# Turning the expert loop of a mixture-of-experts decoder layer by half an item, and loading two weight slices one step sooner

## The chip, the cores and the metric

The kernel runs on one core of a Trainium2 chip. The metric is device time of one execution in microseconds (us). The kernel before took 1735.72 us (median of 3 runs, 1734.24 to 1736.85).

## What is computed

One decoder layer on 512 tokens of width 1024: an attention part (two groups of heads, not touched here), and then a mixture of experts. Each token goes to 4 of 32 experts:

```
logits = h @ w_router + b_router
top_val, top_exp = lax.top_k(logits, TOP_K)          # TOP_K = 4
gate_w = jax.nn.softmax(top_val, axis=-1)
...
gt = jnp.minimum(xb @ w_gate[e] + b_gate[e], SWIGLU_LIMIT)
up = jnp.clip(xb @ w_up[e] + b_up[e], -SWIGLU_LIMIT, SWIGLU_LIMIT)
return (gt * jax.nn.sigmoid(SWIGLU_ALPHA * gt) * (up + 1.0)) @ w_down[e] + b_down[e]
```

The weighted results are added up per token, and a layer norm follows. `w_gate`, `w_up` and `w_down` are 1024 x 1024 float32 for each expert, 12 MB per expert.

## The kernel before

**Items.** The pairs of token and expert are cut into items of up to 32 rows of one expert; in this run there are 82 items. Items with an even number use side A of the weight ring, those with an odd number side B; each side holds the three matrices of one expert. A planner on VectorE fills small tables: `land_i` (which load, in order, an item needs), `perm_i`, `done_i`, `done7_i`, `base_i` (for each load: the expert, the item that uses the slots last, the same in units of `s_gu`, the side), and `ends_i` (the number of items and of pairs of items).

**TensorE** runs per item, written out in this order: eight slices `gate_up` k = 0 to 7 (line 1062), with the bias (line 1056) after k = 0; the transposes of the activations after k = 3; `down` slices q = 0 and 1 of the item before, after k = 5; then k = 6 and 7; then `next_rows`: the transposes of the gathered rows (line 1041) and `slots`, four small matmuls (line 1035); then `down` q = 2 and 3 of the item before (line 1084). The loop (line 1152) has two items in its body and turns around between k = 7 and `next_rows`. `land(m)` (line 1114) reads one number of `land_i` from SBUF into a register of TensorE's sequencer; it stands once ahead of q = 2 (only in the first of the two items), once ahead of k = 0 (in both), and once ahead of q = 0 (first item).

**SyncE** issues all weight loads from one in-order queue. For each load x from 2 on it reads four table values, waits until the slots' last user has passed k = 1 (`s_gu` at `done7`), issues the bias of gate and up (line 460), and then gate and up slices (line 449), each as far as its slot is free, then waits for `down` q = 1, issues the bias of down and the four down slices (line 454).

**GpSimd** issues, for each item, an indirect gather of its rows (line 659) and an indirect scatter that adds its result in DRAM (line 675). Ahead of the loop stand two scatters whose indices all lie out of bounds (`nowhere`, line 666), which stand in for the items 'before the first'; the second waits until the first has landed (`s_sc` at 16). Their order with the first gathers is gather, nowhere, gather, nowhere, gather.

**VectorE and ScalarE** do the activation, the slot values and the row copies of each item. The first gather needs `s_idx`, set at line 1781; the scatters ahead of the loop need `s_tables`, set at line 1754.

Of the kernel before, what the change touches and what calls it, by code (L numbers as in the profile page):

```python
# [12 lines left out]
KC = D // P  # L13
# [8 lines left out]
NE = 32  # L22
# [27 lines left out]
NX = 128  # L50
# [9 lines left out]
def build_layer(nc, a, out):  # L60
    f32, bf16, i32, u32 = mybir.dt.float32, mybir.dt.bfloat16, mybir.dt.int32, mybir.dt.uint32
    ALU, ACT, AX = mybir.AluOpType, mybir.ActivationFunctionType, mybir.AxisListType
    ds = bass.ds
    ctx = ExitStack()
    with ctx:
# [289 lines left out]
        def _(sp):  # L355
# [87 lines left out]
            def gate_up_load(k, e, first, m):  # L443

                dst = arena[:, row_of(first, 2 * k + m), :]
                if type(first) is not int:
                    dst = dst.rearrange("p a n -> p (a n)")
                src = a["w_up" if m else "w_gate"][0, e, k * P:(k + 1) * P, :]
                sp.dma_start(dst, src.rearrange("a p n -> p (a n)")).then_inc(s_wg[k], 16)
# [88 lines left out]
            with sp.Fori(2, NE) as x:  # L538
                e = ds(sp.value_load(perm_i[0:1, ds(x, 1)], min_val=0, max_val=NE - 1), 1)
                done = sp.value_load(done_i[0:1, ds(x, 1)], min_val=1, max_val=NX)  # L540
                done7 = sp.value_load(done7_i[0:1, ds(x, 1)], min_val=8, max_val=7 * NX + 1)
                b = sp.value_load(base_i[0:1, ds(x, 1)], min_val=0, max_val=1)
                first = b * 24
                sp.wait_ge(s_bg, x * 16)
                sp.wait_ge(s_gu, done7)
                bias_load(s_bg, 0, 512, e, ds(b, 1))
                for k in range(KC):
                    if k == KC - 1:
                        sp.wait_ge(s_a, done)
                    elif k > 1:  # L550
                        sp.wait_ge(s_gu, done7 + (k - 1))
                    sp.wait_ge(s_wg[k], x * 32)
                    for m in range(2):
                        gate_up_load(k, e, first, m)
                sp.wait_ge(s_dn, done * 3 + 1)
                sp.wait_ge(s_bd, x * 16)
                bias_load(s_bd, 512, 768, e, ds(b, 1))
                for q in range(4):
                    if q == 3:
                        sp.wait_ge(s_c, done + 1)  # L560
                    elif q > 1:
                        sp.wait_ge(s_dn, done * 3 + q)
                    sp.wait_ge(s_wd[q], x * 16)
                    down_load(q, e, first)
# [12 lines left out]
        def _(pool):  # L577
# [75 lines left out]
            def gather(ready, free):  # L653

                pool.wait_ge(s_idx, ready)
                if free is not None:
                    pool.wait_ge(s_tx, free)
                pool.sem_inc(s_past, 1)
                pool.indirect_dma_start(xg, None, h2_d, bass.IndirectOffsetOnAxis(ap=idx_g, axis=0),  # L659
                                        bounds_check=4 * T - 1, oob_is_err=False).then_inc(s_g, 16)  # L660

            def nowhere(before):

                if before:
                    pool.wait_ge(s_sc, 16 * before)
                pool.indirect_dma_start(acc_d, bass.IndirectOffsetOnAxis(ap=idx_s, axis=0), yb, None,
                                        bounds_check=4 * T - 1, oob_is_err=False, compute_op=ALU.add).then_inc(s_sc, 16)
# [11 lines left out]
            pool.wait_ge(s_zst, 16 * QT)  # L679
            pool.wait_ge(s_zero, 1)  # L680
            pool.wait_ge(s_tables, 1)
            gather(1, None)
            nowhere(0)
            gather(2, 1)
            nowhere(1)
            gather(3, 2)
            n_items = pool.value_load(ends_i[0:1, 0:1], min_val=NE, max_val=NX)
            with pool.Fori(1, n_items) as m:
# [8 lines left out]
        def _(pe):  # L697
# [355 lines left out]
            def gate_up_bias(b):  # L1053

                for j in range(4):
                    nc.tensor.matmul(bank[0][strip(j), :], selp[:, j, :], brow[32:44, b, 0:512], start=False, stop=False)
# [51 lines left out]
            for k in range(KC):  # L1108
                gate_up(0, k, 64 if k >= 4 else 32)
                if k == 0:  # L1110
                    gate_up_bias(0)

            def land(m):
                return pe.value_load(land_i[0:1, ds(m, 1)], min_val=0, max_val=NE - 1)

            def next_rows(m):

                pe.wait_ge(s_g, m * 16 + 32)
                rows_transposed()
                pe.wait_ge(s_oh, m + 3)  # L1120
                pe.wait_ge(s_idx, m + 2)
                slots()

            def gate_up_begins(b, m, at):

                pe.wait_ge(s_urd, m)
                pe.wait_ge(s_bg, at * 16 + 16)
                pe.wait_ge(s_xe, m + 1)
                gate_up(b, 0, at * 32 + 32)
                gate_up_bias(b)  # L1130
                for k in (1, 2, 3):
                    gate_up(b, k, at * 32 + 32)
                activations_transposed(m + 1)
                for k in (4, 5):
                    gate_up(b, k, at * 32 + 32)

            def second_half(b, m, at, at1):
                down_begins(1 - b, at1 * 16 + 16, m, m + 1)
                for k in (6, 7):
                    gate_up(b, k, at * 32 + 32)  # L1140

            def rest_of_down(b, at):
                for q in (2, 3):
                    down(b, q, at * 16 + 16)
            next_rows(0)
            gate_up_begins(1, 1, 1)
            down_begins(0, 16, 1, 2)
            for k in (6, 7):
                gate_up(1, k, 64)
            n_items = pe.value_load(ends_i[0:1, 0:1], min_val=NE, max_val=NX)  # L1150
            n_pairs = pe.value_load(ends_i[0:1, 1:2], min_val=NE // 2, max_val=NX // 2)
            with pe.Fori(1, n_pairs) as i:
                next_rows(i * 2 - 1)
                rest_of_down(0, land(i * 2 - 2))
                at = land(i * 2)
                gate_up_begins(0, i * 2, at)
                at1 = land(i * 2 - 1)
                second_half(0, i * 2, at, at1)
                next_rows(i * 2)
                rest_of_down(1, at1)  # L1160
                after = land(i * 2 + 1)
                gate_up_begins(1, i * 2 + 1, after)
                second_half(1, i * 2 + 1, after, at)
            pe.wait_ge(s_g, n_items * 16 + 16)
            rows_transposed()
            pe.wait_ge(s_oh, n_items + 2)
            pe.wait_ge(s_idx, n_items + 1)
            slots()
            for q in (2, 3):
                down(0, q, 16 * NE)  # L1170
            activations_transposed(n_items + 1)
            down_begins(1, 16 * NE, n_items, n_items + 1)
            for q in (2, 3):
# [198 lines left out]
        def _(dve):  # L1372
# [365 lines left out]
            nc.vector.tensor_scalar(colsb[:, 2:3], start, -1.0, None, ALU.add)  # L1738
            nc.vector.tensor_copy(colsb[:, 3:4], second)
            nc.vector.scalar_tensor_tensor(WP[:, 0:NX], parity, second, Wf, ALU.is_equal, ALU.mult).then_inc(s_selb, 1)  # L1740
            nc.vector.tensor_copy(ends_i[0:1, 1:2], pairs[0:1, :])
            nc.vector.tensor_scalar(ends_i[0:1, 0:1], pairs[0:1, :], 2.0, None, ALU.mult)
            nc.vector.memset(val, 0.0)
            nc.vector.memset(backv, 0.0)
# [4 lines left out]
            nc.vector.tensor_scalar(perm_i[0:1, :], bank[6][0:1, 64 + NX:64 + NX + NE], float(NE), None, ALU.add)  # L1749
            nc.vector.tensor_copy(land_i[0:1, :], bank[6][0:1, 224:224 + NX])  # L1750
            nc.vector.tensor_copy(done_i[0:1, :], bank[6][0:1, 384:416])
            nc.vector.tensor_scalar(done7_i[0:1, :], bank[6][0:1, 384:416], 7.0, 1.0, ALU.mult, ALU.add)
            nc.vector.tensor_copy(base_i[0:1, :], bank[6][0:1, 416:448])
            nc.vector.scalar_tensor_tensor(posr[:, :, 0:NE], bank[5][:, 128:160].unsqueeze(1).to_broadcast([P, QT, NE]), 16.0, cum4,
                                           ALU.mult, ALU.add).then_inc(s_tables, 1)
# [51 lines left out]
            slot_values(2, 3)  # L1807
            one_hot(expert_of(slice(2, 3)))
            n_items = dve.value_load(ends_i[0:1, 0:1], min_val=NE, max_val=NX)
            def body(m, landed):  # L1810
                dve.wait_ge(s_a, m + 1)
                dve.wait_ge(s_pr, m + 1)
                nc.vector.tensor_scalar(gcl, bank[0][:, 0:256], 7.0, None, ALU.min).then_inc(s_gdr, 1)  # L1813
                dve.wait_ge(s_act, m + 1)
                nc.vector.tensor_scalar(ucl, bank[0][:, 256:512], 8.0, -6.0, ALU.min, ALU.max).then_inc(s_urd, 1)
                dve.wait_ge(s_gdr, m + 1)
                dve.wait_ge(s_sig, m + 1)
                nc.vector.tensor_tensor(sgm, gcl, sgm, ALU.mult).then_inc(s_pr, 1)  # L1818
                dve.wait_ge(s_urd, m + 1)
                dve.wait_ge(s_pr, m + 2)  # L1820
                nc.vector.tensor_tensor(sgm, sgm, ucl, ALU.mult).then_inc(s_act, 1)
                moved_on(m + 2, m + 2, m * 2 + 4, m + 1)
                slot_values(m + 3, m * 2 + 5)
                e = expert_of(ds(m + 3, 1))
                one_hot(e)
                dve.wait_ge(s_c, m + 1)
                scatter_indices(m + 3, landed)
            body(0, 32)
            with dve.Fori(1, n_items) as m:
                body(m, m * 16 + 16)  # L1830
                weighted(m + 3, m * 16 + 16)
            moved_on(n_items + 2, n_items + 2, n_items * 2 + 4, n_items + 1)
            scatter_indices(n_items + 3, n_items * 16 + 16)
# [67 lines left out]
```

## Time and profile before

| | |
|---|---|
| median of 3 runs | 1735.72 us |
| the profiled execution | 1734.24 us |
| its span, first to last instruction | 1732.4 us |
| what lies around the span | 1.84 us |
| TensorE busy | 1501.7 us, 87% of the span |
| mean granted TensorE clock | 0.914 of full |
| DMA | 488.94 MB, 282 GB/s over the span |

Times in rows are in us from the span's start unless marked ns. PE is TensorE's matmul, PEld its weight load (LDWEIGHTS), PEldq its sequencer (register, branch and table-load instructions), SPq SyncE's queue. A row names line, engine, operation, what it writes and reads, and the number of instructions. The engine rows by stretch give busy time with the number of instructions in brackets, the granted TensorE clock, the mean busy share of the 16 DMA engines and their GB/s.

### The profile page before, as it was taken

Reading aid. Unit: us, or ns where it says so; the run is one execution under the profiler, and the core shown is the slowest. Engines: PE = TensorE matmul, PEld = TensorE weight load, DVE = VectorE, ACT = ScalarE, POOL = GpSimd, SP = SyncE. Lnnn points to the kernel's source line nnn. Section 1 sums busy time; section 2 is a strip of 40 time slices with the busy share of each in tenths; the row PEclk is TensorE's granted clock in tenths of the full one; section 3 lists DMA queues with packets and bytes.
Section 4 is the critical chain, followed back from the end, with each engine's and each line's share of the span. In section 5 each row is a group of like instructions: output and inputs, shape, how many; then the busy total and the mean of one; then the engine's idle time right before and its main releaser. Section 6 shows DMA issues by size and latency. Waiting matters only on the chain. (4 is left out here: it accounts for less than half of the span.)

```text
span 1732.4 us, 39655 instructions
## 1 busy us (share of the span) xinstructions
PE 1501.7 (87%) x14019; PEld 601.1 (35%) x14020; DVE 623.0 (36%) x2318; ACT 250.7 (14%) x690; POOL 293.8 (17%) x220
## 2 busy tenths in 40 slices
PE   6999989889749966887889997997999998979783
PEld 4444445444413311222233332332333332323221
DVE  1147874655843310221222231331323331313224
ACT  1012265640100000000000000000011000000002
POOL 0010000114411210111121221121222121211111
PEclk9999989989769986998999998998999997979897
DMA  9721246831465999999998799769979869395994
GB/s 345 190 73 49 80 159 249 259 126 79 179 269 200 405 402 408 405 402 403 363 390 302 263 363 404 288 257 404 378 281 343 303 239 375 102 403 177 403 404 162
DMA packets 178905, 488.94 MB, mean 282 GB/s; under 512 B 40375, under 2 KB 59891, under 8 KB 177844
## 3 DMA queue, kind: packets, MB, share of 16 engines
q1 hardware_dynamic: 162740, 471.63, 70.9%
q0 software_dynamic: 16128, 16.82, 4.8%
q8 instruction: 22, 0.36, 0.1%
q14 instruction: 15, 0.12, 0.0%
HBM read 474.60 MB, written 17.96 MB: 284 GB/s over the span
## 5 line engine op out<-in xcount | busy, mean ns | idle before, releaser
L1062 PE MATMUL banks<-arena,master 128*32 128x512 f32 x5248 | 682.8, 633 | 129.0 <-DMA arena<-in_w_up 127.3
L1084 PE MATMUL banks<-arena,master 128*32 128x256 f32 x5248 | 340.0, 389 | 3.4 <-DVE master L1793 2.5
L1813 DVE TENSOR_SCALAR master<-banks 128x256 f32<-128x256 f32 x82 | 34.8, 424 | 798.4 <-PE banks L1062 798.4
L1062 PEld LDWEIGHTS banks<-arena,master 128*32 128x32 f32 x5248 | 149.9, 112 | 431.5 <-DMA arena<-in_w_up 211.7
L659 POOL DMA_INDIRECT master<-moe_input,misc x84 | 93.3, 1110 | 919.0 <-DVE misc L1781 865.7
L1084 PEld LDWEIGHTS banks<-arena,master 128*32 128x32 f32 x5248 | 156.7, 112 | 144.6 <-issue 61.8
L675 POOL DMA_INDIRECT moe_output<-master,misc x82 | 130.2, 1587 | 100.4 <-issue 96.7
L1337 ACT ACTIVATE master<-banks 128x256 f32<-128x256 f32 x82 | 31.4, 383 | 565.7 <-PE banks L1071 565.7
L824 PE MATMUL banks<-arena 128*128 128x512 f32 x256 | 112.6, 595 | 0.0
L1332 ACT ACTIVATE master<-master 128x256 f32<-128x256 f32 x82 | 34.2, 416 | 535.8 <-DVE master L1813 535.8
L1761 DVE TENSOR_SCALAR master<-cbias 128x128 bf16<-128x128 f32 x340 | 95.0, 343 | 44.5 <-issue 44.0
L824 PEld LDWEIGHTS banks<-arena 128*128 128x128 f32 x256 | 47.9, 190 | 60.5 <-issue 59.4
L1515 DVE CUSTOM_DVE_ANT_0 arena<-banks,master 128x128 f32<-128x128 f32 (+3 forms) x96 | 46.0, 480 | 63.4 <-PE banks L912 62.8
L1286 ACT ACTIVATE arena<-arena,misc 128x128 f32<-128x128 f32 (+3 forms) x96 | 53.1, 554 | 61.9 <-DVE misc L1515 61.9
L984 PE MATMUL banks<-arena 128*128 128x512 f32 x128 | 57.5, 607 | 1.5 <-DVE arena L1609 1.5
L922 PE MATMUL banks<-cst,arena 128*128 128x128 f32 x240 | 41.6, 311 | 13.7 <-ACT arena L1294 13.2
L912 PE MATMUL banks<-arena 64*128 64x128 f32 (+3 forms) x192 | 44.0, 538 | 3.5 <-DVE misc L1515 3.2
L1041 PE MATMUL banks<-cst,master 128*128 128x128 f32 x166 | 36.6, 303 | 8.2 <-DMA master<-moe_input,misc 8.2
L1041 PEld LDWEIGHTS banks<-cst,master 128*128 128x128 f32 x166 | 16.8, 141 | 77.0 <-issue 68.7
L1071 PEld LDWEIGHTS banks<-cst,master 128*128 128x128 f32 x164 | 17.0, 145 | 74.9 <-issue 74.5
L922 PEld LDWEIGHTS banks<-cst,arena 128*128 128x128 f32 x240 | 29.3, 156 | 37.9 <-issue 25.7
L1818 DVE TENSOR_TENSOR master<-master 128x256 f32<-128x256 f32 x82 | 34.8, 425 | 18.1 <-ACT master L1332 18.1
(311 smaller groups left out, 1268.1 us busy)
## 6 DMA issues: line engine op xcount, KB each, us to landing
arena<-in_w_gate SPq DMA_DIRECT2D x256, 512.0 KB, 11.7
arena<-in_w_up SPq DMA_DIRECT2D x256, 512.0 KB, 13.9
arena<-in_w_down SPq DMA_DIRECT2D x128, 1024.0 KB, 15.4
arena<-in_w_ada SPq DMA_DIRECT2D x12, 2048.0 KB, 13.2
arena<-in_x SPq DMA_DIRECT2D x2, 2048.0 KB, 8.6
arena<-in_w_in SPq DMA_DIRECT2D x2, 2048.0 KB, 9.9
master<-bias_by_distance SPq DMA_DIRECT2D x16, 256.0 KB, 5.0
arena<-in_w_in SPq DMA_DIRECT2D x8, 256.0 KB, 4.3
```

The source lines that it names most:

```text
L659: pool.indirect_dma_start(xg, None, h2_d, bass.IndirectOffsetOnAxis(ap=idx_g, axis=0), bounds_check=4 * T - 1, oob_is_err=False).then_inc( ...
L675: pool.indirect_dma_start(acc_d, bass.IndirectOffsetOnAxis(ap=idx_s, axis=0), yb, None, bounds_check=4 * T - 1, oob_is_err=False, compute_ ...
L824: last = nc.tensor.matmul(b[:, :], w_in[:, k, where:where + P], hT[:, k, :], start=(k == 0), stop=(k == KC - 1))
L912: nc.tensor.matmul(bank[(2 * s + half) % 3][:, 0:n], lhs, rhs, start=not masked, stop=True).then_inc(s_S, 1)
L922: last = nc.tensor.transpose(bank[3 + half][:, kb * P:(kb + 1) * P], Sb[:, s % 4, half, kb * P:(kb + 1) * P], ident)
L984: last = nc.tensor.matmul(bank[1 + 2 * (q % 2) + n][:, :], mixT[:, k, q * P:(q + 1) * P], w_out[:, k, n * 512:(n + 1) * 512], start=(k == ...
L1041: last = nc.tensor.transpose(bank[2][:, c * P:(c + 1) * P], xg[:, c * P:(c + 1) * P], ident)
L1062: last = nc.tensor.matmul(two(bank[0][strip(j), :]), hTe[:, k % 2, strip(k // 2)], arena[:, 24 * b + 2 * k:24 * b + 2 * k + 2, quarter(j)] ...
L1084: last = nc.tensor.matmul(bank[1][strip(j), 0:256], actT[:, c, strip(q)], DN(b, q, c)[:, quarter(j)], start=(q == 0 and c == 0), stop=(q = ...
L1286: nc.scalar.activation(Sb[:, s % 4, u % 2, 0:n], Sb[:, s % 4, u % 2, 0:n], ACT.Exp, scale=-1.0, bias=umin[:, u:u + 1], accum_out=usum[:, u ...
L1515: nc.vector.tensor_tensor_reduce(out=Sb[:, s % 4, half, 0:n], in0=bank[u % 3][:, 0:n], in1=biases, scale=1.0, scalar=3e38, op0=ALU.add, op ...
L1761: nc.vector.tensor_scalar(OH[:, q, :].rearrange("p (j t) -> p j t", j=4), iota4, posr[:, q, e], backv, ALU.subtract, ALU.is_equal)
```

## The change

- TensorE's loop is turned: it now goes around between `down` q = 3 and `gate_up` k = 0, with the bodies in one function `item_body`. The order of the matmuls is the same as before. Both table reads of an item now stand at its head, ahead of k = 0. The loop goes over one pair less, and the last item stands behind it; three register values are read ahead of the loop.
- SyncE issues the first gate slice of a load as soon as k = 0 is used, then up's; the bias and k = 1 follow once k = 1 is used. The first down slice goes out once `down` q = 0 is used, ahead of the bias of down.
- GpSimd issues both `nowhere` scatters ahead of the first gather.
- `ends_i` gets a third value (one more small VectorE instruction), and the first body of VectorE's item loop waits for one landed scatter and not two.

```diff
-                done7 = sp.value_load(done7_i[0:1, ds(x, 1)], min_val=8, max_val=7 * NX + 1)
+                done7 = sp.value_load(done7_i[0:1, ds(x, 1)], min_val=7, max_val=7 * NX)
                 b = sp.value_load(base_i[0:1, ds(x, 1)], min_val=0, max_val=1)
                 first = b * 24
+                sp.wait_ge(s_wg[0], x * 32)
+                sp.wait_ge(s_gu, done7)
+                gate_up_load(0, e, first, 0)
                 sp.wait_ge(s_bg, x * 16)
-                sp.wait_ge(s_gu, done7)
+                gate_up_load(0, e, first, 1)
+                sp.wait_ge(s_gu, done7 + 1)
                 bias_load(s_bg, 0, 512, e, ds(b, 1))
-                for k in range(KC):
+                for k in range(1, KC):
                     if k == KC - 1:
                         sp.wait_ge(s_a, done)
                     elif k > 1:
-                        sp.wait_ge(s_gu, done7 + (k - 1))
+                        sp.wait_ge(s_gu, done7 + k)
                     sp.wait_ge(s_wg[k], x * 32)
                     for m in range(2):
                         gate_up_load(k, e, first, m)
+                sp.wait_ge(s_dn, done * 3)
+                sp.wait_ge(s_wd[0], x * 16)
+                down_load(0, e, first)
                 sp.wait_ge(s_dn, done * 3 + 1)
                 sp.wait_ge(s_bd, x * 16)
                 bias_load(s_bd, 512, 768, e, ds(b, 1))
-                for q in range(4):
+                for q in range(1, 4):
...
+            for n in range(2):
+                nowhere(n)
             gather(1, None)
-            nowhere(0)
             gather(2, 1)
-            nowhere(1)
             gather(3, 2)
...
+            n_items = pe.value_load(ends_i[0:1, 0:1], min_val=NE, max_val=NX)
+            n_whole = pe.value_load(ends_i[0:1, 1:2], min_val=NE // 2 - 1, max_val=NX // 2 - 1)
+            n_last = pe.value_load(ends_i[0:1, 2:3], min_val=NE - 1, max_val=NX - 1)
+
+            def item_body(m, b):
+
+                land = pe.value_load(land_i[0:1, ds(m, 1)], min_val=0, max_val=NE - 1)
+                back = pe.value_load(land_i[0:1, ds(m - 1, 1)], min_val=0, max_val=NE - 1) * 16 + 16
+                here = land * 32 + 32
+                pe.wait_ge(s_urd, m)
+                pe.wait_ge(s_bg, land * 16 + 16)
+                pe.wait_ge(s_xe, m + 1)
+                gate_up(b, 0, here)
+                gate_up_bias(b)
+                for k in (1, 2, 3):
+                    gate_up(b, k, here)
+                activations_transposed(m + 1)
+                for k in (4, 5):
+                    gate_up(b, k, here)
+                down_begins(1 - b, back, m, m + 1)
+                for k in (6, 7):
+                    gate_up(b, k, here)
                 pe.wait_ge(s_g, m * 16 + 32)
                 rows_transposed()
                 pe.wait_ge(s_oh, m + 3)
                 pe.wait_ge(s_idx, m + 2)
                 slots()
...
                 for q in (2, 3):
-                    down(b, q, at * 16 + 16)
...
+                    down(1 - b, q, back)
+            with pe.Fori(0, n_whole) as i:
+                item_body(i * 2 + 1, 1)
+                item_body(i * 2 + 2, 0)
+            item_body(n_last, 1)
...
-            nc.vector.tensor_copy(ends_i[0:1, 1:2], pairs[0:1, :])
+            nc.vector.tensor_scalar(ends_i[0:1, 1:2], pairs[0:1, :], -1.0, None, ALU.add)
+            nc.vector.tensor_scalar(ends_i[0:1, 2:3], pairs[0:1, :], 2.0, -1.0, ALU.mult, ALU.add)
...
-            def body(m, landed):
+            def body(m):
...
-                scatter_indices(m + 3, landed)
-            body(0, 32)
+                scatter_indices(m + 3, m * 16 + 16)
+            body(0)
```

## Rows read from the trace of the kernel before

**Rows 1.** The page: busy time by engine, and the costliest group of instructions.

```profile
PE 1501.7 (87%) x14019; PEld 601.1 (35%) x14020; DVE 623.0 (36%) x2318; ACT 250.7 (14%) x690; POOL 293.8 (17%) x220
...
L1062 PE MATMUL banks<-arena,master 128*32 128x512 f32 x5248 | 682.8, 633 | 129.0 <-DMA arena<-in_w_up 127.3
```

**Rows 2.** Engines by stretch, in stretches with long waits for weights.

```profile
542.00:857.00 315.00, 252.78 (x2628) 82.79 (x2624) 72.92 (x324) 21.43 (x72) 48.75 (x37) 0.88 1.03 403
...
1029.00:1086.00 57.00, 45.50 (x496) 14.97 (x488) 12.16 (x54) 3.57 (x12) 8.22 (x7) 0.88 1.03 398
```

**Rows 3.** Engines by stretch, just before such stretches begin.

```profile
538.00:540.00 2.00, 2.00 (x24) 0.67 (x24) 1.54 (x8) 0.00 (x0) 1.10 (x1) 1.00 0.00 0
862.00:864.00 2.00, 2.00 (x28) 0.52 (x20) 1.40 (x10) 0.00 (x0) 0.16 (x1) 1.00 0.32 131
```

**Rows 4.** Timeline of TensorE's matmuls, one item.

```profile
1021.75 0.24 PE L1035 MATMUL banks<-cbias,master 128*128 128x6 bf16 x4
1021.93 1.93 PE L1084 MATMUL banks<-arena,master 128*32 128x256 f32 x32
1023.68 1.04 PE L1062 MATMUL banks<-arena,master 128*32 128x512 f32 x8
1024.65 0.39 PE L1056 MATMUL banks<-misc,cst 12*32 12x512 bf16 x4
1024.97 1.07 PE L1062 MATMUL banks<-arena,master 128*32 128x512 f32 x8
...
1033.98 0.24 PE L1035 MATMUL banks<-cbias,master 128*128 128x6 bf16 x4
```

**Rows 5.** Timeline of SyncE's queue in the same item.

```profile
1026.34 0.38 SPq L460 DMA_DIRECT2D misc<-bias_parts  x1
1027.02 0.37 SPq L449 DMA_DIRECT2D arena<-in_w_gate  x1
```

**Rows 6.** TensorE's sequencer (by line) and weight loads (timeline), the same item.

```profile
L1152 PEldq ALU_OP  x1: 32/32/32, 1019.2 to 1019.2; - x1
...
L1152 PEldq FUSED_REGOPS  x1: 68/68/68, 1019.6 to 1019.6; - x1
...
L1114 PEldq FUSED_REGOPS  x2: 51/101/151, 1022.4 to 1022.9; - x2
L1114 PEldq TENSOR_LOAD <-cst x1: 297/297/297, 1022.5 to 1022.5; - x1
...
L1060 PEldq FUSED_REGOPS  x1: 37/37/37, 1023.4 to 1023.4; - x1
...
1021.92 1.45 PEld L1084 LDWEIGHTS banks<-arena,master 128*32 128x32 f32 x32
1023.46 0.35 PEld L1062 LDWEIGHTS banks<-arena,master 128*32 128x32 f32 x8
```

**Rows 7.** Line 1056 in two stretches without waits for weights (four matmuls per item).

```profile
L1056 PE MATMUL banks<-misc,cst x36: 383/385/386, 926.8 to 1024.7; 12*32 12x512 bf16 x36
...
L1056 PE MATMUL banks<-misc,cst x64: 383/385/386, 1215.9 to 1399.4; 12*32 12x512 bf16 x64
```

**Rows 8.** Timelines of VectorE, GpSimd and TensorE as the expert stage begins.

```profile
487.99 0.27 DVE L1754 SCALAR_TENSOR_TENSOR cbias<-banks,arena 128x128 f32<-128x128 f32 x1
490.81 0.20 DVE L1781 TENSOR_SCALAR misc<-cbias 128x1 f32<-128x1 f32 x1
...
492.12 1.24 POOL L659 DMA_INDIRECT master<-moe_input,misc  x1 [28.53 <-issue]
...
498.57 0.69 PE L1041 MATMUL banks<-cst,master 128*128 128x128 f32 x2 [8.19 <-DMA master<-moe_input,misc]
```

**Rows 9.** Line 666, the two scatters ahead of the loop.

```profile
L666 POOL DMA_INDIRECT moe_output<-master,misc x2: 1587/1596/1604, 493.7 to 502.3; - x2
...
DMA to landing us min/median/max: 7.0/7.3/7.7
```

**Rows 10.** Line 675, the 82 scatters of the items: time to landing.

```profile
DMA to landing us min/median/max: 3.2/7.4/9.0
```

More of the change, by code:

```diff
@@ L1111, in _ @@
                     gate_up_bias(0)
-            def land(m):
-                return pe.value_load(land_i[0:1, ds(m, 1)], min_val=0, max_val=NE - 1)
-            def next_rows(m):
+            pe.wait_ge(s_g, 32)
+            rows_transposed()
+            pe.wait_ge(s_oh, 3)
+            pe.wait_ge(s_idx, 2)
+            slots()
+            n_items = pe.value_load(ends_i[0:1, 0:1], min_val=NE, max_val=NX)
[18 more added lines that the diff above has]
+                    gate_up(b, k, here)
                 pe.wait_ge(s_g, m * 16 + 32)
@@ L1122, in next_rows @@
                 slots()
[L1124 to L1142, printed above, removed]
-                for q in (2, 3):
-                    down(b, q, at * 16 + 16)
[L1145 to L1170, printed above, removed]
+                for q in (2, 3):
+                    down(1 - b, q, back)
[3 more added lines that the diff above has]
+            item_body(n_last, 1)
             activations_transposed(n_items + 1)
@@ L1751, in _ @@
             nc.vector.tensor_copy(done_i[0:1, :], bank[6][0:1, 384:416])
-            nc.vector.tensor_scalar(done7_i[0:1, :], bank[6][0:1, 384:416], 7.0, 1.0, ALU.mult, ALU.add)
+            nc.vector.tensor_scalar(done7_i[0:1, :], bank[6][0:1, 384:416], 7.0, None, ALU.mult)
             nc.vector.tensor_copy(base_i[0:1, :], bank[6][0:1, 416:448])
@@ L1826, in body @@
                 dve.wait_ge(s_c, m + 1)
-                scatter_indices(m + 3, landed)
-            body(0, 32)
+                scatter_indices(m + 3, m * 16 + 16)
+            body(0)
             with dve.Fori(1, n_items) as m:
-                body(m, m * 16 + 16)
+                body(m)
                 weighted(m + 3, m * 16 + 16)
```

## The prediction

> **What bounds the kernel now.** I read the page first: TensorE is busy for 1501.7 of 1732.4 us, and its costliest line, the gate and up matmuls, also has the largest wait, 129 us, for weights [rows 1]. So the expert stage is bound by TensorE in one place and by DMA in another, and the second view, the engines by stretch, has to say where. There are seven stretches in which the DMA share stands at 1.03 and TensorE is not fully busy; the first and longest runs from 542 to 857 us, the others (868 to 922, 1029 to 1086, 1155 to 1213, 1404 to 1461, 1506 to 1563, 1596 to 1684) last 54 to 88 us; two of the seven are shown [rows 2]. In them time is set by bytes: what TensorE does sooner or later inside changes nothing. Just before six of the seven the DMA engines stand idle, share 0.00 to 0.02; before the one at 865 they still have 0.32 to do [rows 3]. So such a stretch begins when SyncE's first load goes out, and ends a fixed number of bytes later. Between them TensorE is gapless and sets the pace: an item takes 1033.98 - 1021.75 = 12.23 us [rows 4]. The total is therefore the sum of TensorE-paced stretches and DMA-paced ones, and a change has to be priced by which kind it falls in.
>
> The line of the small bias matmul, four per item, counts the items in TensorE-paced stretches: 36/4 = 9 from 921 to 1027 and 64/4 = 16 from 1211 to 1402 [rows 7]; the same count gives 6 (1085 to 1153), 4 (1460 to 1503), 3 (1562 to 1593), 1 near 863, 1 at 1688, and 2 beside the very first in the loop before 540. That is 42 passages from `down` q = 3 to k = 0 of the next item, 21 ahead of an odd item and 21 ahead of an even one (I followed the parity from the loop's branch, which now runs ahead of even items).
>
> **SyncE's order.** The wait for k = 1 ends at 1024.97 + 1.07 = 1026.04; the bias goes out at 1026.34 and the first gate slice at 1027.02 [rows 4, 5]. With the change the first gate slice needs only k = 0, which ends at 1023.68 + 1.04 = 1024.72, and no bias ahead of it: 1.32 us sooner by the wait and 1027.02 - 1026.34 = 0.68 us by the bias, 2.0 us in all. The next slices don't fall behind: k = 0 and up's k = 0 are 1 MB, over 2.5 us at 403 GB/s [rows 2], and the bias and k = 1 follow within 2.0 us. Six of the seven DMA-paced stretches begin dry, so 6 x 2.0 = 12.0 us. The one at 865 begins while a part of the engines still works on old loads: between 0 and 2.0, taken as 1.0. The other loads are issued behind a queue that is full, and gain nothing; so does the down slice that goes out ahead of its bias, which at that time has gate and up slices queued ahead of it. Queued behind SyncE's new wait on the old bias is only its own next slice; that bias was issued a whole load earlier. Sum: -13.0 (bounds -14 and 0: below 0 only if the stretch doesn't begin with this slice).
>
> **TensorE's loop.** The matmuls and their order stay. What moves is sequencer work: a table read (a register operation, a load of 297 ns, register operations of 151 ns) runs from 1022.4 to about 1023.1, 0.7 us, and going around the loop runs from 1019.2 to 1019.67, 0.5 us [rows 6]. It is hidden as long as matmuls are queued ahead. Going around now happens behind k = 6 and 7, whose matmuls last long; it moves behind `down` q = 2 and 3, whose 32 last 1023.68 - 1021.93 = 1.75 us in all, 55 ns each [rows 4]. How much is still queued there? When the table read begins at 1022.4, the weight loads of `down` still run until 1021.92 + 1.45 = 1023.37, and the first weight load of k = 0 comes at 1023.46, right behind the sequencer's last register operation for it at 1023.4 [rows 6]. So one table read and the waits just fit, and nothing is left over. The second read adds 0.7 us to every passage. Of this 0.22 us is covered, because now the weight load at 1023.46 leads its matmul at 1023.68 by that much: 0.48 us exposed. Ahead of odd items the turn of the loop adds 0.47: 0.95 to 1.0, taken as 0.98. Sum: 21 x 0.48 + 21 x 0.98 = 30.7 us. Bounds: 0 if the queue can hold more; 21 x 0.7 + 21 x 1.2 = 39.9 if the 0.22 us isn't cover. I take the first because the sequencer began the read 0.97 us before the loads of `down` ran out, not sooner, although nothing else kept it. In DMA-paced stretches the same idle time lies inside waits for weights. Nothing is gained where the loop turned before: there it was covered.
>
> A row shows the depth: at 1022.4 about (1023.37 - 1022.4)/0.045 = 21 weight loads and, at 55 ns a piece since 1021.93, 23 matmuls were outstanding, 45 instructions [rows 4, 6]. The Trainium skill (TensorE: Matmul & The Clock Gate, Part 1, on queue depths) gives TensorE's queue as 64 deep. By that rule all 64 instructions of `down` q = 2 and 3 would be queued when it starts at 1021.93, 0.47 us sooner than the trace has the read begin; the trace does not agree, and I go by the trace, but keep the rule's result as a rival.
>
> **GpSimd's order.** The first gather needs `s_idx`, which comes at 490.81 + 0.20 = 491.01; it starts at 492.12, 1.1 us later, and TensorE, idle for 8.19 us, starts at 498.57, 6.45 us after that [rows 8]. No wait is longer in this chain, so the first gather's time passes on in full until the first DMA-paced stretch, and past it, since its start hangs on TensorE's k = 0. Now: tables at 488.26, first `nowhere` 1.1 us later at 489.4; it lands 7.3 us after its start, at 496.7 (these two took 7.0 and 7.7) [rows 8, 9]; the second waits for that, starts 1.1 us later at 497.8, runs 1.6 us to 499.4, and the gather starts some 0.6 us behind it at 500.0. That is 7.9 us late. Bounds: with the shortest landing of any scatter, 3.2 us [rows 10], it is 3.8 us; with 7.7 and a slower hand-over 8.9. The down loads that slow the landing start at the same moment, so I keep 7.3. What is late next is TensorE's first transpose. The second gather gains nothing, since it waits for that transpose.
>
> **VectorE.** The third value of `ends_i` is one instruction on one partition, ahead of a wait of VectorE for TensorE (`s_pos`) that it cannot outlast; the wait for one scatter instead of two is long past. Nothing for both. The three register reads ahead of TensorE's loop run while it waits for the row copy: 0 to 0.5 us, taken as 0.
>
> **Sum,** against the profiled execution's own 1734.24 us (span 1732.4 and 1.84 around it; the median of the runs is 1.5 us above it): 1734.24 - 13.0 + 30.7 + 7.9 = 1759.8 us.
>
> **Rivals.**
> 1. *TensorE's queue hides all of it.* If the sequencer could run further ahead than 1.0 us, by more than 0.7 us at even items and 1.2 at odd ones, the loop costs nothing, and 1734.24 - 13.0 + 7.9 = 1729.1 us: faster. The place is k = 0 of each item; it turns the sign as soon as the mean exposure falls below 5.1/42 = 0.12 us. Against it: the weight load at 1023.46 directly behind the register operation [rows 6].
> 2. *A queue of 64.* The read begins 0.47 us sooner, so the exposures fall to 0.01 and 0.51: 21 x 0.52 = 10.9 us, and 1740.0 us. The skill's page named above has this depth.
> 3. *The early slices don't help* (DMA-paced stretches are held by something other than their first byte, a slow engine among the 16, say): 13.0 us more, 1772.8 us. For it: the uneven end before 865 [rows 3]. Against it: idle engines before the other six.
> 4. *The scatter lands fast:* 1755.7 us. Inside the range of the forecast.
>
> **How the numbers follow.** The forecast 0.62, rival 1 0.13, rival 2 0.12, rival 3 0.13 (rival 4 is part of the first). The forecast's own range is 1749 to 1771, from both ends of the exposure and of the landing. For 8 in 10 it has to reach to rival 2 and part of rival 3, and leave out rival 1: 1738 to 1774. What can be told from no change is 0.2%, 3.5 us about the median 1735.7. Faster: rival 1, 0.12. Same: the rest of rival 1 and the low end of rival 2, 0.06. Slower 0.82.
>
> **What the changed profile would show.** Items in TensorE-paced stretches at 12.7 and 13.2 us in turn in place of 12.23; TensorE idle ahead of k = 0, put down to issue, with both table reads in the gap. SyncE's first gate slice about 0.3 us after k = 0 and 2.0 us sooner against the item. The first gather near 500 us and TensorE's first transpose near 506. The DMA-paced stretches as long as before. I would be wrong if the items still take 12.23 us, if the first `nowhere` lands by 493, or if the waits for weights grow by as much as SyncE starts sooner.

## The result, and the profile after

The changed kernel takes 1762.71 us (median of 4 runs, 1762.42 to 1765.37) against 1734.98 us, 27.7 us more: ratio 1.016, 95% interval 1.0144 to 1.0174. It is slower, and lies 2.9 us above the forecast of 1759.8. Its profiled execution took 1760.31 us with a span of 1758.5.

On the page, TensorE's busy time is as before. The view by line gives three causes of idle time for each group. TensorE's idle time ahead of the gate and up matmuls is 147.8 us and was 129.0 [rows 1]. It was nearly all put down to weights (127.3); now weights are 64.7, and 41.6 is put down to issue (time in which the engine waited for nothing that the profile shows) and 40.5 to the bias:

```profile
PE 1503.2 (85%) x14015; PEld 593.0 (34%) x14020; DVE 621.9 (35%) x2319; ACT 250.7 (14%) x690; POOL 294.1 (17%) x220
...
L1069 PE MATMUL banks<-arena,master 128*32 128x512 f32 x5248 | 674.3, 627 | 147.8 <-DMA arena<-in_w_up 64.7 <-issue 41.6 <-DMA misc<-bias_parts 40.5
```

TensorE's timeline shows it at k = 0 (line 1069, after `down` at 1091), once ahead of an odd item and once ahead of an even one; the brackets give the idle time and its cause:

```profile
1019.54 0.24 PE L1042 MATMUL banks<-cbias,master 128*128 128x6 bf16 x4
1019.72 1.93 PE L1091 MATMUL banks<-arena,master 128*32 128x256 f32 x32
1022.51 1.07 PE L1069 MATMUL banks<-arena,master 128*32 128x512 f32 x8 [0.86 <-issue]
...
1032.84 0.24 PE L1042 MATMUL banks<-cbias,master 128*128 128x6 bf16 x4
1033.02 1.93 PE L1091 MATMUL banks<-arena,master 128*32 128x256 f32 x32
1035.19 1.07 PE L1069 MATMUL banks<-arena,master 128*32 128x512 f32 x8 [0.24 <-issue]
```

From the small matmuls of one item to those of the next it is now 13.30 us (1019.54 to 1032.84) and then 12.68, where it was 12.23 [rows 4]. From `down` q = 2 to k = 0 it is 2.79 and 2.17 us, where it was 1.75. The sequencer's rows ahead of the second of these have both table reads (lines 1130 and 1131) in one row, where there was one [rows 6]:

```profile
L1130 PEldq FUSED_REGOPS  x2: 51/101/151, 1033.5 to 1034.0; - x2
L1130 PEldq TENSOR_LOAD <-cst x1: 296/296/296, 1033.6 to 1033.6; - x1
...
L1131 PEldq TENSOR_LOAD <-cst x1: 296/296/296, 1034.2 to 1034.2; - x1
...
L1131 PEldq SEQ_ASSERT  x1: 18/18/18, 1034.8 to 1034.8; - x1
```

The first still begins 0.7 us after the small matmuls (1033.5 against 1032.84; before it was 1022.4 against 1021.75), so the sequencer runs as far ahead as before, and the work added behind that point comes out as idle time. Ahead of the other k = 0, at 1022.51, the turn of the loop (line 1153) also begins 0.7 us after the small matmuls. The sequencer's last register operation ahead of k = 0 (line 1067) comes 2.2 us after that, where it is 1.6 us without the turn (1033.5 to 1035.1); this is the 0.6 us between the two kinds of item:

```profile
L1153 PEldq ALU_OP  x1: 32/32/32, 1020.2 to 1020.2; - x1
...
L1067 PEldq FUSED_REGOPS  x1: 37/37/37, 1022.4 to 1022.4; - x1
...
L1067 PEldq FUSED_REGOPS  x1: 42/42/42, 1035.1 to 1035.1; - x1
```

SyncE's queue at the same k = 0, and GpSimd's timeline as the expert stage begins (line 673 is `nowhere`, 666 the gather) [rows 5, 8]:

```profile
1036.55 0.36 SPq L449 DMA_DIRECT2D arena<-in_w_gate  x1
1037.19 0.35 SPq L449 DMA_DIRECT2D arena<-in_w_up  x1
1037.84 0.37 SPq L460 DMA_DIRECT2D misc<-bias_parts  x1
```

```profile
488.81 1.77 POOL L673 DMA_INDIRECT moe_output<-master,misc  x1 [25.64 <-DVE cbias L1741]
496.61 1.56 POOL L673 DMA_INDIRECT moe_output<-master,misc  x1 [6.03 <-DMA moe_output<-master,misc]
498.47 1.08 POOL L666 DMA_INDIRECT master<-moe_input,misc  x1 [0.30 <-issue]
```

The first gate slice goes out 1036.55 - 1035.19 = 1.36 us after k = 0 begins; before it was 1027.02 - 1023.68 = 3.34. GpSimd waits 6.03 us between the two scatters. In the DMA-paced stretches the DMA share and the rate are as before, 1.03 and about 400 GB/s [rows 2]:

```profile
547.00:861.00 314.00, 248.56 (x2642) 81.48 (x2636) 72.92 (x324) 21.93 (x74) 49.42 (x37) 0.92 1.03 403
1039.00:1096.00 57.00, 48.78 (x506) 15.48 (x502) 12.16 (x54) 4.07 (x14) 9.35 (x7) 0.88 1.03 396
```

### The profile page after: what moved, and what is told of

Its sections match the earlier page's. It is cut to its first block and busy times, and to the rows that moved or that the text cites. A ratio compares the mean times of both kernels' runs of the same rounds, so it can differ in the third digit from the quotient of the medians.

```text
span 1758.5 us, 39756 instructions
## 1 busy us (share of the span) xinstructions
PE 1503.2 (85%) x14015; PEld 593.0 (34%) x14020; DVE 621.9 (35%) x2319; ACT 250.7 (14%) x690; POOL 294.1 (17%) x220
## 5 line engine op out<-in xcount | busy, mean ns | idle before, releaser
L1069 PE MATMUL banks<-arena,master 128*32 128x512 f32 x5248 | 674.3, 627 | 147.8 <-DMA arena<-in_w_up 64.7
L1069 PEld LDWEIGHTS banks<-arena,master 128*32 128x32 f32 x5248 | 142.8, 111 | 465.9 <-issue 263.9
L1091 PEld LDWEIGHTS banks<-arena,master 128*32 128x32 f32 x5248 | 156.3, 111 | 141.5 <-issue 59.6
L1272 ACT ACTIVATE arena<-arena,misc 128x128 f32<-128x128 f32 (+3 forms) x96 | 53.1, 554 | 61.7 <-DVE misc L1501 61.7
```

The lines of the kernel that those rows point to most:

```text
L1069: last = nc.tensor.matmul(two(bank[0][strip(j), :]), hTe[:, k % 2, strip(k // 2)], arena[:, 24 * b + 2 * k:24 * b + 2 * k + 2, quarter(j)] ...
L1091: last = nc.tensor.matmul(bank[1][strip(j), 0:256], actT[:, c, strip(q)], DN(b, q, c)[:, quarter(j)], start=(q == 0 and c == 0), stop=(q = ...
L1272: nc.scalar.activation(Sb[:, s % 4, u % 2, 0:n], Sb[:, s % 4, u % 2, 0:n], ACT.Exp, scale=-1.0, bias=umin[:, u:u + 1], accum_out=usum[:, u ...
```

## The experiments

Ten kernels were run against the kernel before, whose median was 1735.3 to 1735.9 us in these comparisons.

**SyncE's part alone** (the first part of the change's diff, with `done7_i` at 7 times `done`).

> The kernel before with SyncE's new order of issue alone. My theory: each of the seven DMA-paced stretches begins when the first gate slice goes out, so the gain is what the changed kernel's ledger shows for them without the one passage to k = 0 in each: -3.05 + 1.11 - 1.55 - 1.56 - 1.57 - 1.76 - 1.50 = -9.9 us, about 1725 us. Prediction's own term: -13.0 us, 1722 us. Rival (the wait for weights only moves elsewhere, and the ledger's gains come from the slower items, which give the DMA engines more time): 0 us, 1735 us. Items keep 12.23 us in all cases.

1727.11 us, ratio 0.9948 (0.9935 to 0.9961, which is 6.8 to 11.3 us): 8.2 us faster by the medians, where the prediction had 13.0 and the expectation 9.9. To see where the rest went I compared bytes at the same distance from an item's small matmuls, in the stretch that begins at 1155: 4 to 14 us behind them, and the 22 us after. First the kernel before (small matmuls at 1148.06), then SyncE's part alone (1146.82); the last number is GB/s:

```profile
1152.06:1162.06 10.00, 10.00 (x128) 3.95 (x124) 2.42 (x10) 1.19 (x4) 2.17 (x2) 1.00 0.76 247
1162.06:1184.06 22.00, 22.00 (x258) 7.75 (x250) 6.45 (x32) 1.69 (x6) 5.38 (x4) 1.00 1.04 403
```

```profile
1150.82:1160.82 10.00, 10.00 (x128) 3.98 (x124) 2.42 (x10) 1.19 (x4) 2.16 (x2) 1.00 0.94 315
1160.82:1182.82 22.00, 22.00 (x258) 7.71 (x250) 6.44 (x32) 1.70 (x6) 5.39 (x4) 1.00 1.03 403
```

In the first 10 us it is 3.15 MB against 2.47: 0.68 MB ahead, which at 403 GB/s is 1.7 us, and the lead stays, since afterwards both move 403. This pair of rows has one of the larger leads. Over all six dry starts (stretches that begin with idle DMA engines) the same 10 us hold 3.17 MB on average in the three kernels that have this part and the old loop (this one, without down slices, with one scatter), and 2.56 MB in four with SyncE's old order (before, GpSimd's part, unused read behind k = 7, one scatter first): 0.61 MB, 1.5 us.

What a dry start is worth in time is less again. I took the time from k = 0 of the item in which the loads begin to the small matmuls behind the stalled item (in the kernel before, for example, 1023.68 to 1086.71, 63.0 us), as a mean over the five short dry stretches of each profile:

| SyncE's order | kernels | mean of the five stretches, us |
|---|---|---|
| old | before; GpSimd's part; TensorE's part; its read late; unused read at k = 0; the same behind k = 7; one scatter first | 63.2; 62.5; 62.3; 62.4; 62.8; 62.9; 62.7 |
| new | changed kernel; SyncE's part; without down slices; with one scatter; changed kernel mended | 61.4; 61.7; 61.3; 61.3; 61.5 |

The means of the rows are 62.7 and 61.5 us, and the rows don't overlap: a dry start gains 1.2 us, not 2.0. Five are 6.2 us. The long stretch from 542, taken the same way, gains 0.9 on average, within the spread of the profiles, and what the stretch at 865 gives can't be told from that spread either. The table also bears out that a stretch set by bytes doesn't get longer when TensorE's items do (62.3 to 62.8 with slower items, 62.5 to 63.2 without).

The later slices show a like number. First the kernel before, then SyncE's part alone, each with the gate slices of k = 0 and k = 1:

```profile
1153.33 0.37 SPq L449 DMA_DIRECT2D arena<-in_w_gate  x1
...
1154.48 0.34 SPq L449 DMA_DIRECT2D arena<-in_w_gate  x1
```

```profile
1150.08 0.36 SPq L449 DMA_DIRECT2D arena<-in_w_gate  x1
...
1151.97 0.35 SPq L449 DMA_DIRECT2D arena<-in_w_gate  x1
```

Against the small matmuls the slice of k = 0 goes out at 5.27 and now 3.26 us, 2.0 us sooner, but that of k = 1 at 6.42 and now 5.15, only 1.3 us sooner: in the new order the wait until k = 1 is used, and the bias, stand between the two.

**SyncE's part without the down slices.**

```diff
-                sp.wait_ge(s_dn, done * 3)
-                sp.wait_ge(s_wd[0], x * 16)
-                down_load(0, e, first)
                 sp.wait_ge(s_dn, done * 3 + 1)
                 sp.wait_ge(s_bd, x * 16)
                 bias_load(s_bd, 512, 768, e, ds(b, 1))
-                for q in range(1, 4):
+                for q in range(4):
```

> SyncE's new order for the first gate and up slices and their bias alone; the down slices as before. Theory (the down slices go out into a queue that is full, so their order is worth nothing): the same as with both parts, 1727 us within 2 us. Rival (the down part carries some of the 8 us): 1729 us or more.

1726.32 us, ratio 0.9952 (0.994 to 0.9964). The down slices' new order shows no gain of its own; what is gained comes from the order of the first gate and up slices and their bias.

**GpSimd's part alone** (both `nowhere` ahead of the first gather).

> The kernel before with both out-of-bounds scatters ahead of the first gather, nothing else. Theory: the first gather comes 6.8 us later against the tables and TensorE's first transpose 6.2 us later; item 0 gets 1.4 us back if its clock rises sooner again, so +4.8 us in the end (1739.8 us). If the clock's rise was chance: +6.2. Rival (the delay is taken up by the first wait for weights at 590 us): 0.

1739.85 us, ratio 1.0025 (1.0016 to 1.0035): 4.6 us slower by the medians (2.8 to 6.1 by the interval). The delay of the start is not taken up by the later waits for weights.

**One scatter ahead of the first gather, one behind the second.**

```diff
-            gather(1, None)
             nowhere(0)
+            gather(1, None)
             gather(2, 1)
             nowhere(1)
```

> The kernel before with one out-of-bounds scatter ahead of the first gather and the second left in its place. Theory (the delay is the second scatter's wait for the first's landing, not the issuing): the scatter is over 2.8 us after the tables, just as the gather's indices are ready; the gather starts within 0.5 us of its old place against the tables, total within 1 us of before. Rival (each scatter ahead of the gather costs its share, half of the 4.6 us of both): +2.3 us.

1733.89 us, ratio 0.999 (0.998 to 0.9999): 1.7 us faster by the medians, a little more than the 1 us either way that was expected. GpSimd's timeline of this kernel:

```profile
488.99 1.78 POOL L666 DMA_INDIRECT moe_output<-master,misc  x1 [25.62 <-DVE cbias L1754]
491.69 1.09 POOL L659 DMA_INDIRECT master<-moe_input,misc  x1 [0.92 <-DVE misc L1781]
```

The scatter is over at 490.77 and the gather starts at 491.69, waiting for its indices as before. Issuing a scatter ahead of the gather costs nothing here; what costs is the second one's wait for the first to land.

**TensorE's part alone** (the turned loop and the third value of `ends_i`).

> The kernel before with TensorE's turned loop and the third value of the ends table alone. Theory: items in TensorE-paced stretches take 12.70 and 13.30 us in turn, 42 passages give 21 x 0.47 + 21 x 1.07 = 32.3 us, the three register reads ahead of the loop 0.95 us; together +33 us, 1768 us. Rival (the longer items are partly a matter of SyncE's new order, through semaphores or the queue): well under 33 us, items nearer 12.23.

1765.61 us, ratio 1.0175 (1.0162 to 1.0189, which is 28.1 to 32.8 us): 30.3 us slower, where 33 was expected. SyncE's order has no part in it; the items take 12.7 and 13.3 us here too. Item 1 takes 11.84 us against 11.60, so the register reads ahead of the loop cost 0.2 us here and not the 0.95 of the expectation.

**The same with the second table read under cover.**

```diff
-                back = pe.value_load(land_i[0:1, ds(m - 1, 1)], min_val=0, max_val=NE - 1) * 16 + 16
                 here = land * 32 + 32
...
                 for k in (4, 5):
                     gate_up(b, k, here)
+                back = pe.value_load(land_i[0:1, ds(m - 1, 1)], min_val=0, max_val=NE - 1) * 16 + 16
                 down_begins(1 - b, back, m, m + 1)
```

> As the run with TensorE's part alone, with the second table read moved from the head of the item to just ahead of down q = 0, where a long row of gate and up matmuls is queued. Theory (sequencer work beyond about 1.0 us at the head is exposed, one to one): even items back to 12.23 us, odd ones keep the turn of the loop only, 12.23 + 0.3 to 0.6; the sum 21 x (0.3 to 0.6) + 0.5 = 7 to 13 us, about 1745 us. Rival (a queue of 64, with the exposure due to something in the turned loop other than the reads, such as instruction fetch): little change from the 33 us.

1740.5 us, ratio 1.0032 (1.0019 to 1.0044): 5.2 us over the kernel before, less than the 7 to 13 expected. One line moved past six slices of matmuls takes 25 of 30 us away. The small matmuls of three items in a row:

```profile
1099.67 0.24 PE L1035 MATMUL banks<-cbias,master 128*128 128x6 bf16 x4
1112.16 0.24 PE L1035 MATMUL banks<-cbias,master 128*128 128x6 bf16 x4
1124.39 0.24 PE L1035 MATMUL banks<-cbias,master 128*128 128x6 bf16 x4
```

12.49 us and 12.23: one kind of item is back where it was, the other keeps 0.26 us for the turn of the loop. 21 x 0.26 = 5.5 us, close to the 5.2 measured.

**An unused read ahead of k = 0, in the kernel before**, whose loop is not turned:

```diff
                 at = land(i * 2)
+                land(i * 2 - 1)
                 gate_up_begins(0, i * 2, at)
...
                 after = land(i * 2 + 1)
+                land(i * 2)
                 gate_up_begins(1, i * 2 + 1, after)
```

> The kernel before, nothing turned; one more table read, whose value is not used, stands behind the one that already stands ahead of k = 0 in both items of the loop. Theory (one read and the waits just fit into what is queued of down, a second is exposed): every TensorE-paced item takes 12.70 us in place of 12.23, 42 passages give 42 x 0.47 = 19.7 us, about 1755 us. Rival (a queue of 64, and what is exposed in the changed kernel comes from its turned code): 0 to 0.5 us in all, 1735 us.

1755.68 us, ratio 1.0123 (1.0108 to 1.0138): 20.1 us, where 19.7 was expected. Items take 12.7 to 12.8 us; two of them, and k = 0 between:

```profile
1041.69 0.24 PE L1035 MATMUL banks<-cbias,master 128*128 128x6 bf16 x4
1041.87 1.93 PE L1084 MATMUL banks<-arena,master 128*32 128x256 f32 x32
1044.09 1.06 PE L1062 MATMUL banks<-arena,master 128*32 128x512 f32 x8 [0.29 <-issue]
...
1054.42 0.24 PE L1035 MATMUL banks<-cbias,master 128*128 128x6 bf16 x4
```

**The same unused read behind k = 7:**

```diff
             with pe.Fori(1, n_pairs) as i:
+                land(i * 2 - 1)
                 next_rows(i * 2 - 1)
...
+                land(i * 2)
                 next_rows(i * 2)
```

> The kernel before with the same unused read, but ahead of the transposes, behind k = 6 and 7 of gate and up. Theory (the same work is free where matmuls of 116 ns are queued): items stay at 12.23 us but for the first after a stall, within 2 us of the kernel before. Rival (a table read costs TensorE 0.47 us wherever it stands): 1755 us, as with the read ahead of k = 0.

1737.88 us, ratio 1.0014 (1.0006 to 1.0023): 2.3 us, a little more than the 2 I allowed. Two items of it:

```profile
1023.89 0.24 PE L1035 MATMUL banks<-cbias,master 128*128 128x6 bf16 x4
1036.12 0.24 PE L1035 MATMUL banks<-cbias,master 128*128 128x6 bf16 x4
```

12.23 us: the same two reads per pair of items are free here, and cost 20 us when they stand behind `down` q = 3. Only the first item after some stalls, when TensorE has nothing queued, shows them (12.6 to 12.9 us in place of 12.2 to 12.4, and 14.6 once, for which I have no cause).

**SyncE's part with one scatter ahead of the first gather.**

> The kernel before with the two parts that measured faster or even: SyncE's new order (8 to 9 us faster) and one out-of-bounds scatter ahead of the first gather (0 to 1.7 us faster). Theory (they lie in different places and add up): 1725 to 1727 us, ratio 0.994 to 0.995. Rival (what one gives the other takes): 1730 us or more.

1726.34 us, ratio 0.9944 (0.9931 to 0.9957). With SyncE's part alone it is the same within the intervals, and both beat the kernel before and the changed one.

**The changed kernel mended**: the second read ahead of `down` q = 0, and the scatters in the old order.

> The changed kernel with two of its pieces put back: the second table read stands ahead of down q = 0, and gathers and out-of-bounds scatters go in the old order; the turned loop and SyncE's order stay. Theory (terms add up): 1735.5 - 8.5 for SyncE + 5.2 for the turn of the loop, which keeps 0.26 us at every odd item, = 1732 us. Rival (with the loads sooner something else in the changed kernel comes to the fore): over 1736 us.

1731.97 us, ratio 0.9975 (0.9965 to 0.9984). The expectation's terms make 3.3 us less than the kernel before (8.5 less, 5.2 more), and 3.9 less was measured. The changed kernel was 27.7 us slower than the kernel before; with two small moves it is 3.9 us faster.

## Why the prediction was right

**The terms.** Measured alone, the three parts give -8.2, +30.3 and +4.6 us by the medians, 26.8 in all from the unrounded ones, and the whole change gave 27.7. The prediction had -13.0, +30.7 and +7.9, 25.6 in all.

**TensorE's loop: right, and shown.** The second read cost 0.48 us by the prediction; in the changed kernel the item took 12.70 in place of 12.23 us, 0.47. With the turn it had 0.98 us; 1.07 was measured. That the sequencer's reach ahead of the matmuls is what runs out is shown from three sides: the read alone costs it (20.1 us), the same read under k = 6 and 7 costs next to nothing (2.3), and the changed kernel's own read, moved, gives it back (25 us). The turn of the loop costs 0.26 us once the read is gone, not the 0.47 to 0.5 that its rows last, so here a part still fits. On top of two reads nothing fits, and the 0.60 us is the time by which the sequencer's rows last longer. The 30.7 is nearer to the 30.3 than its parts are: 21 x 0.47 + 21 x 1.07 is 32.3 us, inside the interval but 2 us over the median, and I have no cause for these 2 us.

For the three register reads ahead of the loop I had taken 0. In the changed kernel the way from item 1's small matmuls to its k = 0 is 2.22 us long where it was 1.27, which is 0.95 us more; TensorE waits for 1.97 us of it, put down to issue. The three reads aren't alone in this: behind them, on the sequencer, come item 1's own two table reads, which the kernel before didn't have for this item:

```profile
L1124 PEldq TENSOR_LOAD <-cbias x1: 487/487/487, 513.0 to 513.0; - x1
...
L1131 PEldq SEQ_ASSERT  x1: 18/18/18, 516.8 to 516.8; - x1
```

With TensorE's part alone this item is only 0.2 us longer, so the price depends on what else happens at the start.

**SyncE's order: right in kind, over-sized.** The step was "1.32 us sooner by the wait and 0.68 us by the bias, 2.0 us in all", six times, and 1.0 for the stretch at 865. The first slice does go out 2.0 us sooner, 1.98 in the rows above. The bytes are ahead by 1.5 us on average, and a dry stretch is 1.2 us shorter. The prediction had said that the next slices don't fall behind because the bias and k = 1 follow within 2.0 us. They follow in 1.9 us (1150.08 to 1151.97), but then the slice of k = 1 is only 1.3 us sooner than it was. I had read the lead off the issue of one slice. That the gain ends at the lead of the later slices fits the 1.2, but no kernel tests it: one that issues the bias later, behind k = 1, would.

**GpSimd's order: right in kind, over-sized.** The gather starts 10.64 us behind the tables (498.47 against 487.83), where the prediction had 11.74 and the kernel before has 3.86. The step that was off is "lands 7.3 us after its start ..., starts 1.1 us later": the second scatter starts 7.80 us after the first, not 8.4. The gather's rows then take 5.87 us to TensorE's first transpose, not 6.45. This makes about 6.2 us; 4.6 were measured. In two profiles with this part item 0 was also shorter, 10.27 and 10.49 us against 11.71: the granted clock rose to full sooner (4 to 6 us behind item 0's small matmuls it was 0.90 and 0.79 on average, against 0.50). But in other kernels, with the gather in its old place, item 0 took 10.26, 10.49 and 10.88 us as well, so I don't count it as an effect. Between 4.6 and 6.2 the cause stays open; the interval of the measured price reaches to 6.1.

**What cancelled.** The two over-sized terms have opposite signs: -5.1 us was predicted for both together, -3.6 measured. In part this is luck: the forecast of the total is better than its terms.

**The rivals.** That TensorE's queue hides all of it fell with the items of 12.70 and 13.30 us. The queue of 64 would have given 12.24 and 12.74; the read still begins 0.7 us after the small matmuls, at the same 45 or so outstanding instructions by the prediction's estimate. So the depth in the Trainium skill (TensorE: Matmul & The Clock Gate, Part 1) is not what this kernel's sequencer can use: the trace does not agree. That the early slices don't help fell with SyncE's part alone.

The prediction did not name one more rival: that the sequencer is no further because it is busy, and not because it is held. In the item of [rows 6] the turn of the loop and a table read ahead of `down` q = 2 kept it until 1020.7, 1.0 us before the small matmuls. The item after it, with small matmuls at 1033.98 [rows 4], has neither there; its sequencer is past the last wait ahead of the small matmuls (line 1121) at 1031.7, 2.3 us before them. Yet the read ahead of k = 0 begins 0.65 us behind the small matmuls in both, so the sequencer is held:

```profile
L1114 PEldq TENSOR_LOAD <-cst x1: 310/310/310, 1020.1 to 1020.1; - x1
...
L1121 PEldq EVENT_SEMAPHORE  x1: 51/51/51, 1031.7 to 1031.7; - x1
...
L1114 PEldq FUSED_REGOPS  x2: 51/101/151, 1034.6 to 1035.2; - x2
```

**Which stretch a cost falls in** carried the count. TensorE's longer items cost only in the 42 passages outside the DMA-paced stretches; inside them it lies in waits for weights. Had all 81 passages cost it, TensorE's part would have taken some 62 us more, not 30.3.

## What to carry to other kernels

A register read or a loop's turn on TensorE's sequencer is free only while enough matmul time is queued ahead of it. Put it behind the longest matmuls, not the shortest: the same 0.7 us read, twice per pair of items, cost 2.3 us in all under matmuls of 116 ns and 20.1 us under those of 55 ns. Where a kernel alternates between a bound of bytes and one of an engine, price each edit in the stretch in which it lies; and for a load that starts earlier, look at when its later slices go out, not only its first, and measure the length of the stretch. Two dummy transfers in a row are cheap to issue and dear if the second waits for the first to land.

## What was not expected

The first gate and up slices used to arrive after their bias; now the bias can be last. In the stalled item of the stretch at 1039, TensorE's wait ahead of k = 0 ends with the bias, not with the weights:

```profile
1077.03 1.93 PE L1069 MATMUL banks<-arena,master 128*32 128x512 f32 x8 [3.41 <-DMA misc<-bias_parts]
```

By these rows it costs nothing in the end, since TensorE then waits for the next slices all the same (0.81 us ahead of k = 2, for weights); no kernel tests it. Over the whole profile the wait put down to the bias is 40.5 us, where there was none among the causes before.
